# Three of four token tiles of a product-key expert layer: dense products over all experts in place of gathered rows

## What is computed

```python
qp = (h @ w_pq).reshape(b, s, 8, 2, 128)
sc = einsum("bshpd,hpnd->bshpn", qp, sub_keys)         # two sets of 128 key scores per head
s1, i1 = top_k(sc[..., 0, :], 16)
s2, i2 = top_k(sc[..., 1, :], 16)
cand = (s1[..., :, None] + s2[..., None, :])            # 16 x 16 sums
top_s, top_c = top_k(cand, 16)
expert = i1[top_c // 16] * 128 + i2[top_c % 16]
gate = softmax(top_s)
u = take(peer_u, expert)                                # rows of 1024, table of 64 MB
a = einsum("bcd,bchkd->bchk", h, u)
w = gate * gelu(a)
vv = take(peer_v, expert)                               # rows of 1024, table of 64 MB
y = einsum("bchk,bchkd->bcd", w, vv)                    # sum over 8 heads x 16 experts
x = x + gate2 * y
```

## Time and profile before

| | |
|---|---|
| median of 3 runs | 2909.39 us (2909.04 to 2912.01) |
| span of the profiled execution | 2948.8 us, first to last instruction |
| its own time beyond the span | not recorded; the span alone is 39.4 us over the median |
| busy in the span: PE, DVE, ACT, POOL | 2315.5, 1562.3, 735.2, 1233.2 us |
| read from HBM | 640.78 MB |
| mean granted TensorE clock | 0.934 |

### The profile page before, as it was taken

How to read it: one execution, slowest core, us unless ns; L and a number is a source line. 1 busy time by engine, 2 the same in 40 slices (tenths; PEclk the granted TensorE clock), 3 DMA queues, 4 the chain that set the end, 5 groups by cost and what they waited for, 6 DMA issues and landing times.

```text
span 2948.8 us, 30187 instructions
## 1 busy us (share of the span) xinstructions
PE 2315.5 (79%) x8606; PEld 1370.8 (46%) x8606; DVE 1562.3 (53%) x3743; ACT 735.2 (25%) x1504; POOL 1233.2 (42%) x1158
## 2 busy tenths in 40 slices
PE   8999789999989699998766666676666666666668
PEld 6877677777779378743222222222222222222223
DVE  5535656542354554375655555555555556555551
ACT  4334322222235355112112111111212111111112
POOL 0001101100000001055767776677676777776674
PEclk9999989999999899999988998989898999998899
DMA  4100025642212010276988988888897989898797
GB/s 180 58 29 1 1 93 192 229 153 83 100 67 77 15 44 1 86 242 251 352 308 319 345 314 320 317 333 329 316 359 284 342 330 354 317 343 318 297 354 284
DMA packets 167023, 644.19 MB, mean 218 GB/s; under 512 B 18816, under 2 KB 19072, under 8 KB 157840
## 3 DMA queue, kind: packets, MB, share of 16 engines
q0 software_dynamic: 154656, 563.68, 51.6%
q1 hardware_dynamic: 11232, 77.60, 7.5%
q10 hardware_dynamic: 1040, 1.67, 0.2%
HBM read 640.78 MB, written 2.10 MB: 218 GB/s over the span
## 4 chain that ended last, share of the span: by engine, by line
PE 43%; issue 17%; DMA 13%; POOL 11%; DVE 10%; ACT 3%; DVEq 2%; ACTq 1%; POOLq 0%; PEldq 0%; another core or an unknown queue 0%; PEld 0%
PE ps L1522 8%; DMA big<-peer_v,r 7%; PE ps L1476 6%; DMA r<-peer_u,r 6%; PE ps L1718 6%; PE ps L1392 5%; POOL big L432 5%; PE ps L1544 4%; POOL r L432 4%; PE ps L1687 4%; DVE r L1322 3%; POOL r L422 2%; PE ps L1457 2%; PE ps L1661 1%; PE ps L1429 1%
## 5 line engine op out<-in xcount | busy, mean ns | idle before, releaser
L1718 PE MATMUL ps<-big,r 128*128 128x512 f32 x2048 | 1075.7, 661 | 503.2 <-DMA big<-peer_v,r 395.6
L1718 PEld LDWEIGHTS ps<-big,r 128*128 128x128 f32 x2048 | 388.6, 207 | 1190.4 <-issue 839.0
L1322 DVE CUSTOM_DVE_ANT_0 r<-r 128x1024 f32<-128x1024 f32 x512 | 622.3, 1225 | 554.3 <-DMA r<-peer_u,r 509.2
L432 POOL DMA_INDIRECT big<-peer_v,r x512 | 568.4, 1110 | 184.5 <-issue 140.4
L432 POOL DMA_INDIRECT r<-peer_u,r x512 | 528.4, 1032 | 177.2 <-issue 138.0
L778 ACT ACTIVATE r<-const,r 128x128 f32<-128x128 f32 x512 | 192.2, 397 | 1092.6 <-PE ps L1718 438.9
L1476 PE MATMUL ps<-w_lo,h_hi 128*128 128x256 f32 x544 | 154.5, 284 | 0.0
L918 DVE TENSOR_TENSOR w_lo<-big,w_hi 128x2048 fp32r<-128x2048 f32 x42 | 96.2, 2290 | 106.2 <-ACT w_hi L538 106.2
L369 POOL CAST w_hi<-big 128x2048 fp32r<-128x2048 f32 x4 | 8.0, 2012 | 340.6 <-ACTq L728 280.4
L1392 PE MATMUL ps<-big 128*128 128x256 f32 (+1 forms) x656 | 147.8, 380 | 0.3 <-issue 0.3
L1522 PE MATMUL ps<-h_hi,w_hi 128*128 128x512 f32 x352 | 141.1, 401 | 8.2 <-issue 4.7
(11 more groups left out here) (267 smaller groups left out, 3167.3 us busy)
## 6 DMA issues: line engine op xcount, KB each, us to landing
big<-wst SPq DMA_DIRECT2D x70, 1024.0 KB, 5.0
r<-wada POOLq DMA_DIRECT2D x48, 512.0 KB, 4.6
r<-peer_u,r POOLq DMA_INDIRECT x512
big<-peer_v,r POOLq DMA_INDIRECT x512
x<-x_in SPq DMA_DIRECT2D x4, 512.0 KB, 7.0
out<-x SPq DMA_DIRECT2D x4, 512.0 KB
r<-subk_in POOLq DMA_DIRECT2D x1, 1024.0 KB, 7.0
r<-rope_in ACTq DMA_DIRECT2D x1, 640.0 KB, 9.0
```

Of the source, the lines that this page charges most:

```text
L432: pool.indirect_dma_start(rows[k % ROWS], None, (peer_u, peer_v)[kind], bass.IndirectOffsetOnAxis(ap=stage[kind][:, k:k + 1], axis=0)).the ...
L1322: v.tensor_tensor_reduce(out=urows[k % ROWS], in0=urows[k % ROWS], in1=h2[:, t, :], scale=1.0, scalar=0.0, op0=ALU.mult, op1=ALU.add, accu ...
L1718: mm = pe.matmul(ps[:, b + half, :], diag[:, k % 4, :], vrows[k % ROWS][:, 512 * half:512 * half + 512], start=False, stop=False, skip_gro ...
```

## The change

Tiles 0 to 2 (`DT` = 3, `DN` = 384 tokens) no longer gather. Their gates become dense: for each tile an array of gates, 16384 experts by 128 tokens. It is built from one-hot products. For each token, `one1` is a matrix of 128 slots (8 heads x 16) by 128 first keys with a one at the slot's first key, `one2` the same for the second key times the slot's gate, and one matmul over the slots gives the token's 128 x 128 gates. ACT writes them to a staging area of 64 KB a partition (`stage`), and SP stores each tile to a tensor `gd` in device memory, in four DMAs of 2 MB; the next tile's writes to `stage` wait for them (`stage_free`).

Then all 16384 experts are computed for the 384 tokens in 128 steps of 128 experts. Experts of step j are the rows j, 128 + j, 256 + j, ..., so that one DMA reads 128 rows of 4 KB that lie 512 KiB apart. The u rows are transposed in two halves through one PSUM bank, split into high and low parts (ACT, then DVE), and multiplied by the transposed h2 in three passes. Gelu results of 16 steps (`AHEAD`) are kept in a ring; 16 of the steps' hidden parts are done ahead, among the one-hot products. A step's weights are gate times gelu, split again, and three passes with the split v rows add to three tiles' outputs, which stay in six PSUM banks for the whole loop.

The fourth tile still gathers 128 u and 128 v rows, now with three buffers of each kind, spread over steps 4 to 112 of the loop. Its sums are made by DVE, without PE. Its choosing is also spread over these steps. The choosing itself changes: of the 16 x 16 sums only 136 that can be among the best 16 are made, and the operations of the two key sets alternate, with one drain for both. DVE chooses tiles 0 to 2 while the query products run. h2 is laid out with tokens on partitions for the fourth tile alone.

```diff
+DT = T - 1
+DN = DT * P
+NE = NKEYS
+AHEAD = 16
+CHUNK = 8
+NCH = P // CHUNK
+UR, VR, GB, RW = 3, 3, 4, 3
+NCAND = 16 + 15 * 8
+FIRST_ROW, LAST_ROW = 4, 112
...
         @block.sync
+            def load_u(j):
+                if j >= UR:
+                    sp.wait_ge(u_tr, 2 * (j - UR) + 2)
+                sp.dma_start(uraw[:, j % UR, :], u_by_key[:, j, :]).then_inc(u_load[j % UR], 16)
+            def load_v(i):
+                if i >= VR:
+                    sp.wait_ge(v_acc, i - VR + 1)
+                sp.dma_start(vraw[:, i % VR, :], v_by_key[:, i, :]).then_inc(v_load[i % VR], 16)
...
+            store_gates(2)
+            sp.wait_ge(g_acc, 2 * DT * NCH)
...
+            for i in range(NE):
+                if i + AHEAD + 2 < NE:
+                    load_u(i + AHEAD + 2)
+                if i + VR < NE:
+                    load_v(i + VR)
+                if i % GB == GB - 1 and i // GB + 2 < NE // GB:
+                    load_gates(i // GB + 2)
         @block.gpsimd
+            for kind, n in rows3:
+                rows, got, done, table = ((urows, u_in, u_row, peer_u), (vrows, v_in, v_row, peer_v))[kind]
+                if kind == 0 and n % TOPK == 0:
+                    pool.wait_ge(idx_ready, n // TOPK + 1)
+                if n >= RW:
+                    pool.wait_ge(done, n - RW + 1)
+                pool.indirect_dma_start(rows[n % RW], None, table, ...).then_inc(got[n % RW], 16)
         @block.scalar
+            for t in range(DT):
+                stage_free(act, t)
+                for c in range(NCH):
+                    for half in range(2):
...
+                        act.activation(stage[:, :, at:at + 4].rearrange("p e t -> p t e"),
+                                       ps[:, 4 + n % 4, :].rearrange("p (t e) -> p t e", t=4), ACT.Copy).then_inc(g_ev, 1)
+                    if c % 4 == 3:
+                        j = 2 + 4 * t + c // 4
+                        u_high(2 * j + 1)
+                        u_high(2 * j + 2)
+                        gelu(j)
...
+            for i in range(NE):
+                gelu(i + AHEAD - 1)
+                u_high(s + 1)
+                w_high(i + 1)
+                v_high(i + 1)
+                u_high(s + 2)
         @block.vector
+            def tile_picks(t):
+                v.tensor_copy(topf.rearrange("p a h k -> p (a h k)"), topi[:, t, :])
+                pair_ranks(besti[:, t, :], rank_bits, ranks, wrap)
+                for a in range(2):
+                    v.tensor_tensor(hot, over(ranks[:, a, :], TOPK), each(iota, SLOTS), ALU.is_equal)
+                    v.tensor_tensor(hk, hk, topf[:, a].unsqueeze(2).broadcast_to([P, PH, TOPK, TOPK]), ALU.mult)
+                    v.tensor_reduce(picks[:, t, a, :], hot, AX.X, ALU.add)
...
+            for h in range(PH):
+                v.wait_ge(sk_ev, 2 * h + 2)
+                for t in range(DT):
+                    key_tops(t, h)
+                    pair_tops(t, h).then_inc(top_done, 1)
+            for s in range(3):
+                u_low(s)
+            for t in range(DT):
+                tile_picks(t)
...
+                for c in range(NCH):
+                    v.tensor_tensor(one1[:, n % 2], each(keys, CHUNK), over(slotT[t][...], NKEYS), ALU.is_equal)
+                    for k in range(CHUNK):
+                        v.tensor_scalar(one2[:, n % 2, k, :], keys, slotT[t][:, P + at:P + at + 1],
+                                        slotT[t][:, 2 * P + at:2 * P + at + 1], ALU.is_equal, ALU.mult)
+                    if n and n % 4 == 0:
+                        j = 1 + n // 4
+                        u_low(2 * j + 1)
+                        u_low(2 * j + 2)
...
+            for i in range(NE):
+                w_mul(i + 1)
+                u_low(s + 1)
+                w_low(i + 1)
+                v_low(i + 1)
+                for n in todo[:1]:
+                    row3(n)
+                u_low(s + 2)
+                for n in todo[1:]:
+                    row3(n)
+                for h, part in tops_at(i):
...
         @block.tensor
+            def u_transposes(s):
+                if half == 0:
+                    pe.wait_ge(u_load[j % UR], 16 * (j // UR + 1))
+                if s:
+                    pe.wait_ge(u_lo_done, s)
+                for k in range(KD // 2):
+                    mm = pe.transpose(ps[:, 1, P * k:P * k + P], uraw[:, j % UR, at:at + P], ident)
+            def hidden(s):
+                pe.wait_ge(u_lo_done, s + 1)
+                for k in range(KD // 2):
+                    for i, (w, h) in enumerate(passes((uT_hi[:, s % 2], uT_lo[:, s % 2]), (hd_hi, hd_lo))):
+                        mm = pe.matmul(ps[:, 0, 0:DN], w[:, k, :], h[:, KD // 2 * half + k, :], ...)
+            def experts_out(i, tiles):
+                pe.wait_ge(v_lo_done, i + 1)
+                pe.wait_ge(ew_lo_done, i + 1)
+                for t in tiles:
+                    for half in range(2):
+                        for n, (vv, w) in enumerate(passes((v_hi[:, i % 2], v_lo[:, i % VR]), (ew_hi[:, i % 2], ew_lo[:, i % 2]))):
+                            mm = pe.matmul(ps[:, 2 + 2 * t + half, :], w[:, P * t:P * t + P], vv[:, 512 * half:512 * half + 512], ...)
...
+            for i in range(NE):
+                s = 2 * (i + AHEAD)
+                if i + AHEAD < NE:
+                    u_transposes(s + 1)
+                    experts_out(i, [0])
+                    hidden(s)
+                    u_transposes(s + 2)
+                    experts_out(i, [1, 2])
+                    hidden(s + 1)
+                else:
+                    experts_out(i, [0, 1, 2])
```

## The result

| | before | after |
|---|---|---|
| median of 4 runs | 2909.22 us (2900.91 to 2912.01) | 2836.36 us (2835.0 to 2838.61) |
| ratio | | 0.9769, 95% interval 0.9743 to 0.9796 |
| span of the profiled execution | 2948.8 us | 2834.8 us |
| granted TensorE clock, mean | 0.934 | 0.957 |

The change makes the kernel 2.3% faster. The forecast was 2830 us, the measurement 2836. The page of the kernel after says first where the work now lies: busy time of each engine, bytes, and the chain that ended last by engine.

The account below looks back on a forecast made before the run. The expert stage was taken as bound by gathered bytes. Loop start 1714, full steps 1064, last steps 70 and end 10.5 summed to 2859 us, times 0.987 2821, taken as 2830; range 2780 to 2895, 8-in-10 2745 to 3000.

Parts of the forecast that it names:

- The choosing: Before the one-hot products: DVE picks for three tiles, ending at 1443 us, with TensorE waiting some 80 us.
- The dense gates: One-hot products after choosing: 12 groups of 16.9 us, 203 us, plus 32 of store stalls and 36 before the loop.
- The loop: 112 full steps paced by TensorE at 9.5 us each, 1064 us, from 1714 to 2778 us.
- the margin of 0.3 for block boundaries: In each loop step: 9.2 us of TensorE work taken as 9.5, for four block boundaries.
- Last steps: After the full loop: 16 steps without hidden products, TensorE 4.14 us taken as 4.4 each, 70 us.
- What must stay below it: In a loop step, other engines fit under TensorE's 9.5 us: DVE 7.6, ACT 3.4, DMA 2.5 MB at 262 GB/s.
- the sign of being wrong: In the loop: PE waiting for u or v loads or low u, with TensorE idle over 1 us a step.
- From the profiled execution to the runs: Whole kernel: median is 0.987 of the span, 39 us added by profiling, so 2859 gives 2821; 2830 taken.
- (1) DMA: Rival: gathers and strided loads make the loop DMA bound, 11.9 us a step at 210 GB/s, 3087 us; chance 0.15.
- (2) DVE and the ring of waits: Rival: u's turns through PE, ACT, DVE make loop steps 10.5 us, 2932 us, slower by 0.8%; chance 0.12.
- (3) Dearer stages before the loop: Rival: two-pointer operations at 0.40 us and stores at 210 GB/s give 2944 us, no change; chance 0.08.
- (4) Less overlap lost: Rival: loop steps of 9.2 us and gates of 162 us give 2748 us; chance 0.08.

Follow-up runs that it names:

- The four experiments on a step: Four edits of the changed kernel: no fourth-tile rows 2826.43 us, contiguous u and v loads 2835.82, one more DVE operation a step 2872.13, two passes of hidden products 2718.11.
- 24 added operations: Changed kernel with an extra 1.15 us DVE operation only in the 24 steps holding part of the fourth tile's choosing: 2864.03 us.
- halved bytes: Changed kernel without the fourth tile's rows (no gathers, row products or row sums): 2826.43 us.
- one operation a step more: Changed kernel with one more 1024-column DVE operation, result unused, before the low half of v in each step: 2872.13 us.

## Why the prediction was right, and where only its sum was

**The choosing** was to end at 1443 us; the first one-hot comparison starts at 1448.9. A head of one tile took DVE 5.39 us for 5.3 and its last selection ended at 1384, not 1376; the three tile_picks took 51 us for 52. TensorE's gap was there, 15 busy of 89 us.

**The dense gates.** Two-pointer operations are 0.34 us long and 0.26 apart (eight in 2.13), for 0.37 and 0.29. A group took 16.1 us for 16.9. All 48 chunks took 190 us besides the stalls (1448.9 to 1668.4), for 203; eleven groups had low halves in them, not twelve. The two stalls at stores were 29.7 us together (the first 15.37) for 32, and from the last one-hot to the loop 41.5 us passed for 36, 19.07 of them the wait for u. The loop starts at 1709.9 for 1714: errors of +6, -13, -2 and +5 us cancel to -4, which is luck. ACT's strided writes took 1.06 us each, near the doubling that was allowed, and stayed hidden.

**The loop** was sized too long: 112 steps took 1045.3 us for 1064. An undisturbed step is 9.25 us for 9.5, which is 28 us; late steps gave back 9.7 of them. The cadences themselves made 9.2; the margin of 0.3 for block boundaries is hardly there (behind four transposes the second output matmul starts 0.31 us after the first and not 0.23, the others at the usual distance, when their data are ready). Last steps: 4.18 for 4.4. The end of 10.5 us came out so. The four experiments on a step agree with TensorE as the pace of an undisturbed step.

**What must stay below it.** DVE had 6.95 us a step (750.1 us in 108 steps) for 7.6. The slack was described as if each step had it and "the next step gives the delay back". That failed in the steps with choosing: three in a row leave nothing to give back, and 24 added operations cost 28 us, a part of it by the clock. In the kernel as it is this is worth 8 us of TensorE's idle time, 0.08 a step where over 1 was to be the sign of being wrong.

**From the profiled execution to the runs.** The factor 0.987 was wrong. The step took the 39 us between span and median as something that the kernel after would have too. They belonged to one slow execution's gathers; the kernel after has a span of 2834.8 and a median of 2836.4. The sum of 2859 was 24 us too high, the factor took 38 off, and 9 were put back by choosing 2830. The forecast lies 6 us off by luck: two errors of opposite sign nearly cancel, the sum's 24 (the loop 19, its start 4) and the 29 that were taken off for profiling; the sum alone would have been 0.8% off. The mechanism, TensorE's cadence as the pace of a loop with all else below it, is what the runs bear out.

**The rivals.** (1) DMA: refuted by halved bytes, -10 us, and by contiguous loads, 0. (2) DVE and the ring of waits: not the pace; it shows in seven late steps, 10 us in all, and is close: one operation a step more is 36 us. (3) Dearer stages before the loop: the loads and stores were not slow (336 to 383 GB/s in the stalls, against a bound of 210). (4) Less overlap lost: its 9.2 was the nearer for an undisturbed step (9.25); the mean of 9.33 lies half way to 9.5, and the gates' 190 us are nearer to 203 than to its 162.

## What to carry to other kernels

Where gathered rows bound a stage, a dense product over a whole table can be cheaper although it does many times the arithmetic; its price is TensorE's cadence times its matmuls. Once a loop is TensorE's, look for gains ahead of it: half-size staging in two buffers took 40 us and no arithmetic, four times what leaving away a whole tile's gathers gave. An engine's slack is to be counted in the worst run of steps, not as a mean, and a late step can cost more than its wait, since matmuls behind a wait of 4.4 us ran at half rate for a while; a spare engine is no spare if it holds a neighbour up. And before the difference between a span and the median is taken for a property of the kernel, a second profile of the same kernel should show it.

## What the runs showed of the hardware

A POOL product of 128x2048 fp32 took 4.5 us where DVE didn't hold it up (1399.58 to 1404.08), where DVE's took 2.29, and stretched DVE operations of 0.29 us to 3.95 and 4.43. A u load of 512 KB behind 8 MB of stores on one queue took 20.8 us to land, for a median of 7.4. Loads of 128 pieces of 4 KB at a pitch of 512 KiB landed as soon as contiguous ones (7.4 and 5.3 against 7.5 and 5.3 us). Stores of 2 MB, four in flight, went at 336 to 343 GB/s together with the loads of u beside them.

Evacuations from PSUM written with a stride took ACT 1.06 us for the same 512 columns that contiguous ones take in 0.60 (one line of ACT in the kernel after; ns min/median/max):

```profile
L896 ACT ACTIVATE big<-ps x96: 1025/1058/1117, 1453.4 to 1670.6; 128x512 f32<-128x512 f32 x96
```
